# A two-block network on one core: each half of a product leaves PSUM ahead of the split of the same half of a later weight block

## What is computed

```python
def sandwich_ffn(x, w_gate_up, w_down, g_pre, g_post, shift, scale, gate):
    h = modulate(rms_norm(x, g_pre), shift, scale)
    return x + 0.5 * gate * rms_norm(swiglu(h, w_gate_up, w_down), g_post)
...
def second_block(...):
    for i in range(DEPTH_2):
        ...
        x = layer_norm(ALPHA * x + h, ln_g[i, 0], ln_b[i, 0])
        x = layer_norm(ALPHA * x + sq_relu_mlp(x, mlp_w1[i], mlp_w2[i]), ln_g[i, 1], ln_b[i, 1])
        x = x + jax.nn.sigmoid(x @ ple_w_gate[i]) * (p[i] @ ple_w_proj[i])
```

## Time and profile before

| | us |
|---|---|
| median of 3 runs (lowest, highest) | 3643.77 (3637.68, 3647.68) |
| the profiled execution | 3642.33 |
| its span, first to last instruction | 3640.7 |
| TensorE matmul busy | 3239.5 (89%) |
| DVE busy | 1711.2 (47%) |
| ACT busy | 1383.8 (38%) |
| mean granted TensorE clock | 0.937 of 2.4 GHz |

### The profile page before, as it was taken

The page is one execution under the profiler, slowest core; times in us unless marked ns, Lnnn a source line. Parts: engine busy times, 40 slices in busy tenths (PEclk is TensorE's granted clock), DMA queues, the critical chain, the costliest instruction groups (busy, mean ns, idle before and its releaser), DMA issues. The chain is left out here.

```text
span 3640.7 us, 51756 instructions
## 1 busy us (share of the span) xinstructions
PE 3239.5 (89%) x20836; PEld 2793.0 (77%) x20836; DVE 1711.2 (47%) x2536; ACT 1383.8 (38%) x2225; POOL 195.1 (5%) x289
## 2 busy tenths in 40 slices
PE   4999979889999799989799779986899989887998
PEld 2777757557778588757599668975799879886897
DVE  2332262553323532254655436655564566553665
ACT  2322232432222322232454425543453545452553
POOL 1111014001110000003000000000000000000000
PEclk9999989899999899999899869997899999996999
DMA  6455334035554223324155314642165445441452
GB/s 213 156 168 162 105 107 116 12 100 167 161 171 130 81 93 101 121 90 131 47 173 185 122 51 129 195 136 92 56 191 182 152 123 186 156 148 49 136 189 92
DMA packets 403048, 471.08 MB, mean 129 GB/s; under 512 B 9660, under 2 KB 380940, under 8 KB 402858
## 3 DMA queue, kind: packets, MB, share of 16 engines
q1 hardware_dynamic: 379120, 388.00, 33.6%
q0 software_dynamic: 22880, 80.12, 7.1%
q10 hardware_dynamic: 858, 0.29, 0.0%
HBM read 467.20 MB, written 1.20 MB: 129 GB/s over the span
## 5 line engine op out<-in xcount | busy, mean ns | idle before, releaser
L420 DVE TENSOR_TENSOR w_lo<-w_raw,w_hi 128x1024 fp32r<-128x1024 f32 x734 | 893.0, 1227 | 1517.2 <-ACT w_hi L417 1517.1
L428 PE MATMUL bank<-a_hi,w_hi 128*128 128x256 f32 (+1 forms) x3864 | 1241.1, 321 | 136.8 <-DVE a_lo L1488 38.6
L417 ACT ACTIVATE w_hi<-w_raw 128x1024 fp32r<-128x1024 f32 x734 | 767.9, 1057 | 1541.2 <-PE bank L430 1471.8
L429 PE MATMUL bank<-a_lo,w_hi 128*128 128x256 f32 (+1 forms) x3864 | 1228.3, 318 | 0.0
L430 PE MATMUL bank<-a_hi,w_lo 128*128 128x256 f32 (+1 forms) x3864 | 1226.3, 317 | 0.0
L428 PEld LDWEIGHTS bank<-a_hi,w_hi 128*128 128x128 f32 x3864 | 741.4, 192 | 218.2 <-issue 119.0
L430 PEld LDWEIGHTS bank<-a_hi,w_lo 128*128 128x128 f32 x3864 | 741.0, 192 | 50.8
L429 PEld LDWEIGHTS bank<-a_lo,w_hi 128*128 128x128 f32 x3864 | 740.7, 192 | 48.5 <-issue 0.5
L428 PE MATMUL bank<-h_hi,w_hi 128*128 128x256 f32 (+1 forms) x1728 | 548.3, 317 | 0.0
L429 PE MATMUL bank<-h_lo,w_hi 128*128 128x256 f32 (+1 forms) x1728 | 541.6, 313 | 0.0
L430 PE MATMUL bank<-h_hi,w_lo 128*128 128x256 f32 (+1 forms) x1728 | 541.2, 313 | 0.0
(11 more groups left out here) (263 smaller groups left out, 2495.8 us busy)
## 6 DMA issues: line engine op xcount, KB each, us to landing
w_raw<-in_mlp_w SPq DMA_DIRECT2D x128, 1024.0 KB, 5.5
w_raw<-in_w_ffn_gate_up SPq DMA_DIRECT2D x88, 1024.0 KB, 5.1
m_raw<-in_w_mod POOLq DMA_DIRECT2D x130, 512.0 KB, 4.8
w_raw<-in_w_ffn_down SPq DMA_DIRECT2D x32, 1024.0 KB, 6.3
w_raw<-in_gla_w_in SPq DMA_DIRECT2D x24, 1024.0 KB, 5.3
w_raw<-in_w_in SPq DMA_DIRECT2D x16, 1024.0 KB, 5.7
w_raw<-in_ple_w_gate SPq DMA_DIRECT2D x16, 1024.0 KB, 5.2
w_raw<-in_w_ffn_down SPq DMA_DIRECT2D x16, 768.0 KB, 5.6
```

What stands on the lines that cost most here:

```text
L417: e.activation(hi, raw, ACT.Copy).then_inc(S.hi_ready.sem, 1)
L420: e.tensor_tensor(lo, raw, hi.bitcast(F32), ALU.subtract).then_inc(S.lo_ready.sem, 1)
L428: e.matmul(dst, hi, rhs_hi, start=start, stop=False)
L429: e.matmul(dst, hi, rhs_lo, start=False, stop=False)
```

## The change

`cut`, `ahead` and all eviction functions take the halves that they are to do. In `gemm` the last block of a pair now does: evict half 0, split half 0 of block n+2, evict half 1, split half 1 of block n+2. The other blocks of a pair are as before. A modulation column is turned behind that and no longer ahead of the evictions. `cut_hidden` of the squared relu is called once for the pair behind both halves (`after`). The semaphore values that each eviction waits for are the same. The remaining hunks give `copy_to`, `residual_to_z`, `gated` and `times_c` the argument `ms` in the same way.

```diff
@@ -401,11 +401,11 @@
                     e.wait_ge(S.lo_ready.sem, count)
                 e.dma_start(dst, s).then_inc(landed[n % RAW], 16)
-            def cut(m, i=None, step=0):
+            def cut(m, i=None, step=0, halves=(0, 1)):
                 if total and m >= total[0]:
                     return
-                for half in range(2):
+                for half in halves:
                     c = slice(half * P, half * P + P)
                     raw, hi, lo = w_raw[:, m % RAW, :, c], cut_slot(w_hi, m)[:, :, c], cut_slot(w_lo, m)[:, :, c]
                     if act:
...
@@ -419,9 +419,9 @@
                         e.wait_ge(S.hi_ready.sem, val(2 * m + half + 1, i, 2 * step))
                         e.tensor_tensor(lo, raw, hi.bitcast(F32), ALU.subtract).then_inc(S.lo_ready.sem, 1)
-            def ahead(n, i, step):
-
-                cut(n + CUT, i, step)
+            def ahead(n, i, step, halves=(0, 1)):
+
+                cut(n + CUT, i, step, halves)
             def three(dst, hi, lo, rhs_hi, rhs_lo, start, stop):
...
@@ -539,7 +539,7 @@
                 return mod[:, o:o + 2 * DK].rearrange("p (k s) -> p k s", s=2)
-            def gemm(w, kgs, pairs, per, rhs, evict, by, mod_per=0, first_col=0, sums=None, between=None):
+            def gemm(w, kgs, pairs, per, rhs, evict, by, mod_per=0, first_col=0, sums=None, between=None, after=None):
...
@@ -579,11 +579,17 @@
                                               ready if p == 0 and i is None else None)
                             if sums and g == 0 and p:
                                 sums(p - 1)
-                            ahead(n, i, step)
+                            if g < len(kgs) - 1:
+                                ahead(n, i, step)
+                            else:
+                                for m in range(2):
+                                    evict(i, p, per, lambda m: val(2 * n + 1 + m, i, 2 * step), b, (m,))
+                                    ahead(n, i, step, (m,))
                             if mod_per:
                                 mod_turn(i, p * mod_per + g, per * mod_per)
                             n += 1
-                        evict(i, p, per, lambda m: val(2 * n - 1 + m, i, 2 * step), b)
+                        if after:
+                            after(i, p, per)
                         if between:
                             next(between, None)
                 width = rhs(0)[0].shape[-1]
...
@@ -686,10 +692,10 @@
                             e.tensor_tensor(dst, dst, b[m][:, 0:n], ALU.add).then_inc(S.dve_evicted.sem, 1)
                 return evict
-            def residual_to_z(i, p, per, used, b):
+            def residual_to_z(i, p, per, used, b, ms):
                 if dve:
-                    for m in range(2):
+                    for m in ms:
                         e.wait_ge(S.slot_used.sem, used(m))
                         c = (2 * p + m) * TT
                         e.scalar_tensor_tensor(out=part(z_f, c, i, 2 * per * TT, T), in0=part(xt_f, c, i, 2 * per * TT, T),
...
@@ -1358,21 +1364,21 @@
                 base = Counts(a=S.act_evicted.n, d=S.dve_evicted.n, h=S.hidden_hi.n, l=S.hidden_lo.n)
-                def squared_relu(i, p, per, used, b):
+                def squared_relu(i, p, per, used, b, ms):
                     if act:
-                        for m in range(2):
+                        for m in ms:
                             e.wait_ge(S.slot_used.sem, used(m))
                             e.wait_ge(S.dve_evicted.sem, val(base.d + 2 * p - 1 + m, i, 2 * per))
                             e.activation(tmp_g[:, m, 0:T], b[m][:, 0:T], ACT.Relu).then_inc(S.act_evicted.sem, 1)
                     if dve:
-                        for m in range(2):
+                        for m in ms:
                             e.wait_ge(S.act_evicted.sem, val(base.a + 2 * p + m + 1, i, 2 * per))
                             e.wait_ge(S.hidden_hi.sem, val(base.h + 2 * p - 1 + m, i, 2 * per))
                             e.wait_ge(S.hidden_lo.sem, val(base.l + 2 * p - 1 + m, i, 2 * per))
                             e.tensor_tensor(tmp_y[:, m, 0:T], tmp_g[:, m, 0:T], tmp_g[:, m, 0:T], ALU.mult).then_inc(S.dve_evicted.sem, 1)
-                    cut_hidden(i, p, per, T, (base.d, base.h))
-
-                gemm(A["mlp_w1_2"][i], [(0, DK)], 16, 4, a_op(T), squared_relu, S.act_evicted)
+
+                gemm(A["mlp_w1_2"][i], [(0, DK)], 16, 4, a_op(T), squared_relu, S.act_evicted,
+                     after=lambda i, p, per: cut_hidden(i, p, per, T, (base.d, base.h)))
                 for s in (S.dve_evicted, S.hidden_hi, S.hidden_lo):
                     s.n += 32
                 at.lag = (2, 2)
```

More of the change, by code:

```diff
@@ L676, in to_z, with evict @@
             def to_z(n, add=False):
-                def evict(i, p, per, used, b):
-                    for m in range(2):
+                def evict(i, p, per, used, b, ms):
+                    for m in ms:
                         dst = part(z_f, (2 * p + m) * TT, i, 2 * per * TT, n)
@@ L1452, in ple, with gated @@
                 base = Counts(a=S.act_evicted.n, d=S.dve_evicted.n, v=S.dve.n)
-                def gated(i, p, per, used, b):
-                    for m in range(2):
+                def gated(i, p, per, used, b, ms):
+                    for m in ms:
                         if act:
@@ L1857, in conv, with times_c @@
                 ready = S.act_evicted.n
-                def times_c(i, p, per, used, b):
+                def times_c(i, p, per, used, b, ms):
                     if dve:
                         e.wait_ge(S.act_evicted.sem, ready)
-                        for m in range(2):
+                        for m in ms:
                             e.wait_ge(S.slot_used.sem, used(m))
```

## The result

The changed kernel takes 3603.26 us (median of 4 runs, 3601.42 to 3605.05) against 3645.72 us (4 runs) for the kernel before: a ratio of 0.989, 95% interval 0.987 to 0.991. The prediction was 3606. The profiled execution of after took 3601.42 us, 40.9 us less than that of before. Two executions of all that this document reports, one of before (6517.48 us) and one of the changed kernel (8291.26 us), were far slower than the rest and are in no median here.

The account below looks back on a forecast made before the run. It took the order in which ACT and DVE empty their queues behind each stage's last product as the bound. Terms (a) to (h) summed to 36.9 us, giving 3606 us from 3643.77; forecast 3598 to 3614, range 3595 to 3620.

Parts of the forecast that it names:

- (b): Out projection of each layer, 4 ends: transposes and split of `p` start sooner, 2.9 us each, 11.6 us in all.
- (c): Feed-forward blocks over 512 tokens into post_norm, 3 ends: squares on ACT start sooner, 5.4 us in all.
- (f): `r_gate` product of gla, 2 ends: one split falls behind the last eviction, 0.95 us less each, 1.9 us.
- (a): `mlp_w2` into layer norm, 4 ends: subtraction of the mean 1.79 us sooner, held by `w_lo`, 7.2 us in all.
- rival 2: The clock: all column sums behind the longer pause at half clock, costing 9.5 us, 3615 or 3616; 13 in 100.
- (d): First part of 512-token feed-forward blocks into the second, 3 ends: gate_up waits less for ACT evictions, 5.1 us in all.
- (e): Ple product into the next layer, 3 ends: next input's first split `a_lo` comes 1.25 us sooner, 3.8 us in all.
- (g): Stages with squares and evictions both on ACT (`w_out` twice, last feed-forward block): one eviction goes, 1.1 us in all.
- (h): Conv, where DVE is full: only the first pair's two evictions of 0.37 us fill a wait, 0.75 us.
- the first (splits come too late, slower): Splits behind evictions make TensorE wait at each `mlp_w1` block, costing 47 us, 3653 us; 4 in 100.
- a sign of being wrong: The forecast would be wrong if a new TensorE wait for `w_lo` appeared inside a stage.
- The third: Gain stays in the queue, `border` waits now in the open behind `w_lo`: 14 us lost, 3620 us; 9 in 100.

Follow-up runs that it names:

- the two later profiles: The changed kernel, unaltered, run twice more beside other kernels: 3606.13 us (3640.13 for before) and 3605.98 us (3644.36 for before).
- the matmuls put in the pause: Changed kernel plus 14 constant 128x128 matmuls on TensorE ahead of each layer norm's column sums, result unused: 3594.72 us, ratio 0.988 to before.
- the `mlp_w2` one: Kernel before with the new order only in the four `mlp_w2` stages, all other stages in the old order: 3634.82 us, ratio 0.997.
- The kernels of the first experiment: Against the kernel before: new order only at each stage's last pair, 3603.8 us, ratio 0.988; only at all other pairs, 3645.96 us, ratio 1.001.
- a split worth 12 us more: Changed kernel with the second half's last split, or its `w_lo`, issued behind the step the next stage needs: 3593.97 us, ratio 0.987 to before.
- the one with `residual_to_z` alone: Kernel before with the new order only where the eviction is `residual_to_z` (out projections and `mlp_w2`): 3628.0 us, ratio 0.994.

## Why the prediction was right, and where it was not

The total was 3 us off, and that is partly luck. In the first profile (b) and (c) gave 4.3 us more than forecast and (f) 3.7 us less; attention gave 2.9 us that were not forecast; and beside other runs of before the gain was 34.0 and 38.4 us, not 42.5. Part by part:

- **(a), right, with the clock as forecast in size.** The queue gives the 1.79 us exactly in three layers, 1.92 in the fourth. Behind it the time from the subtraction to the reciprocal is 9.38 and 9.42 us in two of the four norms and 10.24 and 10.29 in the others, before 9.5 to 9.7: the longer pause costs half a microsecond now and then, within the bound of 9.5 us that rival 2 put on it. In the two later profiles it costs nothing (9.3 to 9.6 us), and the four gaps shrink by 8.2 and 8.5 us instead of 6.6. The rule quoted from the Trainium skill (TensorE: Matmul & The Clock Gate, section "Why this matters for your kernels") bears more than I gave it: I wrote that it left little to lose, and that is so for this change, but the matmuls put in the pause show 11.4 us to win by it. Nor is its figure what the rows show: the sums of the earlier trace rows ran at 0.50 behind a pause of 2.30 us.
- **(b), right mechanism, term too small.** I took 2.9 us an end between 2.56 and 3.16. The transposes ran at the full clock, so the `p` split came 3.16 us sooner in layer 0, the upper bound, and 3.0 to 3.4 us in the others. I also overlooked that the subtraction had waited between the end of `a_lo` and its own start, since TensorE's sums stood behind the slow transposes; now it follows `a_lo` without a pause. The subtraction came 3.17 to 3.52 us sooner (13.5 together), and the column sums gave 1.1 more: 14.6 measured, against 11.6.
- **(c), 6.6 against 5.4.** The queue did as forecast: the squares start 0.96 us behind the last `w_hi` instead of 3.00, 2.04 sooner, and 1.51 sooner in the first block, where the modulation column stands ahead of them (1.4 forecast). What I had left out is the clock again: the column sums of the last tiles, first in before, then in after, with the squares ahead of them:

```profile
1201.80 2.40 PE L766 MATMUL bank<-tmp_g,ones 128*128 128x512 f32 x4 [2.86 <-ACT tmp_g L759]
```
```profile
1186.26 1.13 ACT L765 ACTIVATE tmp_g<-z 128x512 f32<-128x512 f32 x2
1186.93 1.98 PE L772 MATMUL bank<-tmp_g,ones 128*128 128x512 f32 x4 [0.81 <-ACT tmp_g L765]
```

  A pause of 0.81 us in place of 2.86, and the two sums in 1.98 us at a granted clock of 1.00, in place of 2.40 us at 0.80 (before, in the first block, 2.58 us).
- **(d), (e), (g)** came as forecast, within 0.3 us each over all their ends. **(h)** gave 0.6 us against 0.8, but not by the step that I named: the gap is the same 9.84 us in the kernel with the new order at last pairs alone, whose first conv pair is in the old order. And one kernel with conv wholly in the old order, the `mlp_w2` one, shows 9.89. What moves it isn't shown.
- **(f), wrong.** I forecast 0.95 us less at each end of the gate product of gla. From the end of `k_low` (L1572, now L1578), which releases ACT at the start of this product, to the first matmul of the chunks (L1596, now L1602) it is 17.69 and 17.68 us before and 18.59 and 18.60 after, and 18.59 in both later profiles of the changed kernel: 0.9 us more each, 1.8 us together. (The rest of the 2.7 us in the result lies ahead of `k_low`. From the making of `g_rank`, L1528, it takes 48.8 to 50.6 us to get there, in kernels of either order.) The step that failed was to treat the stage as free in its interior. ACT and DVE before, then after, at the first block of the gate product:

```profile
2093.19 2.02 ACT L417 ACTIVATE w_hi<-w_raw 128x1024 fp32r<-128x1024 f32 x2 [4.68 <-DVE k_low L1572]
...
2094.35 2.36 DVE L420 TENSOR_TENSOR w_lo<-w_raw,w_hi 128x1024 fp32r<-128x1024 f32 x2 [1.25 <-ACT w_hi L417]
...
2095.22 1.28 ACT L705 ACT_TABLE_LOAD   x1
2096.51 0.66 ACT L705 ACTIVATE r_gate<-bank 128x256 f32<-128x256 f32 x2
```
```profile
2072.18 1.28 ACT L711 ACT_TABLE_LOAD   x1 [4.67 <-DVE k_low L1578]
2073.47 0.39 ACT L711 ACTIVATE r_gate<-bank 128x256 f32<-128x256 f32 x1
2073.75 1.05 ACT L417 ACTIVATE w_hi<-w_raw 128x1024 fp32r<-128x1024 f32 x1
...
2074.91 2.37 DVE L420 TENSOR_TENSOR w_lo<-w_raw,w_hi 128x1024 fp32r<-128x1024 f32 x2 [2.80 <-ACT w_hi L417]
```

  ACT comes late here and is waited for. Before, it made `w_hi` at once, and the table load of 1.28 us for the eviction followed. Now the table load and an eviction stand ahead of `w_hi`, so DVE idles 2.80 us where it idled 1.25, and its decay steps behind `w_lo`, which release ACT again, move back by 1.6 and then 1.9 us. The kernels of the first experiment separate the two effects. With the new order at the last pair alone the 17.7 us become 16.73 and 16.76: 0.95 us less, as forecast. With the new order at all others they become 19.53 twice: 1.85 us more. So the end gave what I said, and the order inside the stage took twice that. Here TensorE also came to wait for a `w_lo`, once a layer, where it never had before:

```profile
PE bank L428 <- DVE w_lo L420: 0.8, 2, 0.4
```

- **Attention, not forecast.** I set all other stages to 0; the two long stretches of the first block's attention shrink by 1.58 and 1.28 us. The kernel with last pairs only shows the same (1.60, 1.26), so it is an end of a stage; with all but the last pairs the stretches stay long (90.68, 65.81 us). Which instruction there was late I haven't traced.
- **The dense stages**: the prediction said that they keep 0.117 us a matmul. They have two values, below; before and after have two slow layers each, so none of the difference between their profiles rests on them, but a median of a few runs can be off by several us through them.

Of the rivals, the first (splits come too late, slower) happened only in gla: the two waits of 0.4 us for `w_lo` above, a thing that the prediction had named as a sign of being wrong, are the only ones, and evictions in the interior moved nothing measurable overall. The third, that the gain stays in the queue behind `border`, fell too, as L1326 follows `w_lo` at once. The second was real but small; it is the largest thing that was left to gain.

## What to carry to other kernels

Where in-order queues serve both the stage that ends and the one that is being prepared, the order of their work matters only at the end of a stage: put what the next step waits for first there, and then ask again what stands ahead of it (here a split worth 12 us more). Within a stage that hides it all, leave the order alone, and above all don't move a step with a table load ahead of something that another engine waits for, where ACT is late. If TensorE has to pause for some microseconds ahead of short matmuls on the path, give it constant matmuls to do.

## What the runs showed of the hardware that I had not expected

The same stream of matmuls (128x128 weights, 256 columns, a weight load each) runs at one of two paces, both at a granted clock of 1.00. In stretches of 90 us inside `mlp_w1` of layers 0 and 1 of before, then of layers 0 and 1 of after, then layer 0 of the changed kernel's second profile (length, TensorE busy and matmuls, weight loads, DVE, ACT, GpSimd, clock, DMA share, GB/s):

```profile
2250.00:2340.00 90.00, 90.00 (x797) 90.00 (x796) 60.71 (x90) 50.80 (x89) 0.00 (x0) 1.00 0.63 196
2640.00:2730.00 90.00, 90.00 (x767) 90.00 (x766) 60.94 (x94) 51.67 (x92) 0.00 (x0) 1.00 0.62 189
```
```profile
2230.00:2320.00 90.00, 90.00 (x767) 90.00 (x766) 57.24 (x83) 47.34 (x82) 0.00 (x0) 1.00 0.59 186
2620.00:2710.00 90.00, 90.00 (x797) 90.00 (x796) 59.93 (x89) 50.58 (x88) 0.00 (x0) 1.00 0.63 198
```
```profile
2230.00:2320.00 90.00, 90.00 (x797) 90.00 (x796) 59.90 (x91) 50.52 (x89) 0.00 (x0) 1.00 0.64 199
```

797 or 767 matmuls in 90 us are 0.113 or 0.117 us each. A whole `mlp` stage pair takes 183.4 or 187.0 us by it, and `mlp_w1` of the same layer and kernel is at one pace in one execution and at the other in the next. The pace also changes inside a stage while TensorE is never idle. Layer 3 of before takes 183.4 us; in its `mlp_w1` and the first block of its `mlp_w2` there are 796 matmuls in 90 us, but later in `mlp_w2` they stand 0.117 us apart. The change stands at the first column sum of a pair (L793), a float32 matmul among the others; the first row is the stretch of 90 us, the other two are the sum and the product behind it:

```profile
3430.00:3520.00 90.00, 90.00 (x796) 90.00 (x795) 60.92 (x91) 52.06 (x90) 0.00 (x0) 1.00 0.63 198
```
```profile
3528.05 0.59 PE L793 MATMUL bank<-tmp_g,ones 128*128 128x256 f32 x2
3528.30 0.47 PE L428 MATMUL bank<-h_hi,w_hi 128*128 128x256 f32 x1
```

Before it the starts lie 0.113 us apart, behind it 0.118. Of 16 changes of pace in the trace of before, 14 stand where two starts lie 0.27 to 0.32 us apart. In the profiles there are 2 slow layers of 4 (187 us) in before, 2, 0 and 2 in the three of the changed kernel, 4 and 3 in the two of the kernel with both evictions first, 4 in the one with `residual_to_z` alone, 0 in the one with all but the last pairs. The last feed-forward block of the first block has two values as well: 183.9 to 184.6 us, and 189.0 in the `mlp_w2` kernel. For the four layers that is up to 14.5 us between executions, a third of what this change is worth. Whether an order of instructions favours one pace can't be told from one profile each, and what sets it stays open: no run tries it apart.
